# Two-layer hybrid trunk on one core: the big tiles of on-chip memory laid out in another order

## What is computed

```python
for l in range(DEPTH):                                   # DEPTH = 2
    x = x + 0.5 * swiglu(rmsnorm(x, ffn1_norm[l]), ffn1_w_gate[l], ffn1_w_up[l], ffn1_w_down[l])
    h = rmsnorm(x, mix_norm[l])
    proj = (h @ w_in[l]).astype(f32)
    z, xbc, dt_raw, q_raw, f_raw, i_raw, g_raw = jnp.split(proj, split_idx, axis=-1)
    y_ssd = ssd_mixer(z, xbc, dt_raw, ...)               # depthwise conv, chunked scan, gated norm
    y_hg = hgrn2_mixer(q_raw, f_raw, i_raw, g_raw, ...)  # gated linear recurrence by chunks
    x = x + jnp.concatenate([y_ssd, y_hg], axis=-1) @ w_out[l]
    x = x + 0.5 * swiglu(rmsnorm(x, ffn2_norm[l]), ffn2_w_gate[l], ffn2_w_up[l], ffn2_w_down[l])
return rmsnorm(x, final_norm)
```

## Time and profile before

| what | value |
|---|---|
| time, median of 3 runs | 2141.71 us |
| the three runs | 2128.27, 2141.71, 2146.33 us |
| the profiled execution: its own time | 2141.71 us |
| the profiled execution: its span | 2140.0 us |
| instructions of the span | 28388 |

### The profile page before, as it was taken

How to read it: one execution, slowest core, us unless ns; L and a number is a source line. 1 busy time by engine, 2 the same in 40 slices (tenths; PEclk the granted TensorE clock), 3 DMA queues, 4 the chain that set the end, 5 groups by cost and what they waited for, 6 DMA issues and landing times.

```text
span 2140.0 us, 28388 instructions
## 1 busy us (share of the span) xinstructions
PE 2093.1 (98%) x10300; PEld 1690.6 (79%) x10300; DVE 813.7 (38%) x1274; ACT 661.6 (31%) x903; POOL 848.1 (40%) x362
## 2 busy tenths in 40 slices
PE   8999999979999999999999999999899999999998
PEld 6888888856678888888888888887567788888887
DVE  7222211774477422221132222119645873222112
ACT  4322223422234322222332222224223342222232
POOL 4444444421123344444444444444211243444444
PEclk9999999988899999999999999999989999999999
DMA  4322232211111222233322223322101122222332
GB/s 146 111 97 92 90 100 91 91 49 40 35 55 60 89 98 92 94 93 99 103 90 98 98 97 92 98 77 89 50 32 49 59 80 89 98 92 95 98 92 95
DMA packets 55812, 181.61 MB, mean 85 GB/s; under 512 B 8368, under 2 KB 10416, under 8 KB 55728
## 3 DMA queue, kind: packets, MB, share of 16 engines
q1 hardware_dynamic: 55728, 180.52, 26.0%
HBM read 178.40 MB, written 2.10 MB: 84 GB/s over the span
## 4 chain that ended last, share of the span: by engine, by line
PE 91%; DVE 6%; issue 2%; DMA 0%; ACT 0%; SPq 0%; DVEq 0%; ACTq 0%
PE ps L1209 28%; PE ps L1210 27%; PE ps L1211 27%; PE ps L1367 3%; DVE acc L826 1%; PE ps L1406 1%; PE ps L1409 1%; PE ps L1459 1%; DVE xs L865 1%; PE ps L1462 1%; PE ps L1224 0%; DVE b L829 0%; DVE b L833 0%; DVE t L824 0%; PE ps L1484 0%
## 5 line engine op out<-in xcount | busy, mean ns | idle before, releaser
L412 POOL TENSOR_TENSOR wlo<-raw,whi 128x1024 fp32r<-128x1024 f32 x348 | 845.7, 2432 | 1280.7 <-ACT whi L445 717.3
L1209 PE MATMUL ps<-hhi,whi 128*128 128x512 f32 x1840 | 739.6, 402 | 0.2 <-issue 0.2
L1210 PE MATMUL ps<-hlo,whi 128*128 128x512 f32 x1840 | 727.2, 395 | 0.0
L1211 PE MATMUL ps<-hhi,wlo 128*128 128x512 f32 x1840 | 726.2, 395 | 0.0
L1209 PEld LDWEIGHTS ps<-hhi,whi 128*128 128x128 f32 x1840 | 352.0, 191 | 83.5 <-issue 9.5
L1211 PEld LDWEIGHTS ps<-hhi,wlo 128*128 128x128 f32 x1840 | 351.8, 191 | 75.3
L1210 PEld LDWEIGHTS ps<-hlo,whi 128*128 128x128 f32 x1840 | 351.9, 191 | 69.8
L445 ACT ACTIVATE whi<-raw 128x1024 fp32r<-128x1024 f32 x168 | 177.3, 1055 | 448.9 <-PE ps L1211 448.9
L1209 PE MATMUL ps<-ahi,whi 128*128 128x512 f32 x704 | 273.9, 389 | 0.0
L1210 PE MATMUL ps<-alo,whi 128*128 128x512 f32 x704 | 273.9, 389 | 0.0
L1211 PE MATMUL ps<-ahi,wlo 128*128 128x512 f32 x704 | 273.9, 389 | 0.0
(11 more groups left out here) (225 smaller groups left out, 1518.1 us busy)
## 6 DMA issues: line engine op xcount, KB each, us to landing
raw<-in_up SPq DMA_DIRECT2D x168, 512.0 KB, 3.2
raw<-in_mix SPq DMA_DIRECT2D x66, 512.0 KB, 3.3
raw<-in_dn SPq DMA_DIRECT2D x64, 448.0 KB, 3.3
raw<-in_dn SPq DMA_DIRECT2D x32, 512.0 KB, 3.5
raw<-in_lead SPq DMA_DIRECT2D x12, 512.0 KB, 3.2
stage<-in_x SPq DMA_DIRECT2D x4, 512.0 KB, 7.0
out<-stage SPq DMA_DIRECT2D x8, 256.0 KB, 2.9
raw<-in_mix SPq DMA_DIRECT2D x4, 256.0 KB, 2.5
```

Source lines behind the costliest of these rows:

```text
L412: pool.tensor_tensor(wlo[:, q, :], raw[:, q, :], whi[:, q, :].bitcast(F32), ALU.subtract).then_inc(split.sem, 1)
L1209: mm(dst, whi[:, q, s], mh, start=start, stop=False)
L1210: mm(dst, whi[:, q, s], ml, start=False, stop=False)
L1211: return mm(dst, wlo[:, q, s], mh, start=False, stop=stop)
```

## The change

The tile x is allocated ahead of hhi, and the arena behind all the other tiles instead of between hlo and x. Nothing else is edited. All lines of the file behind the arena's new place stand one line higher up: L1209 becomes L1208, and so on.

```diff
+        x = sb("x", [P, KD, T])
         hhi = sb("hhi", [P, KD, T], F32R)
         hlo = sb("hlo", [P, KD, T], F32R)
-
-
-        REGION = 27 * 1024 + 256 + 62 * 1024
-        arena = sb("arena", [P, REGION // 4])
-        base = nc.sbuf_base - REGION
-
-        x = sb("x", [P, KD, T])
         raw = sb("raw", [P, NS, BW])
         whi = sb("whi", [P, NS, BW], F32R)
         wlo = sb("wlo", [P, NS, BW], F32R)
...
         ntn = sb("ntn", [P, 2, TC * 8])
         headsum = sb("headsum", [P, NP * 8])
+
+
+        REGION = 27 * 1024 + 256 + 62 * 1024
+        arena = sb("arena", [P, REGION // 4])
+        base = nc.sbuf_base - REGION
```

## The result

The changed kernel took 2153.55 us in the median of 11 runs (2144.57 to 2166.11), the kernel before 2136.51 us in 11 runs (2128.27 to 2146.79). The ratio is 1.0067 with a 95% interval of 1.0042 to 1.0093: slower by 14 us on 2136.51, with 9 to 20 us as the interval. The two medians of 11 lie 17.0 us apart; over all 24 runs of the changed kernel on record, these 11 among them, the median is 2150.16 us, which is 13.7 above 2136.51. The forecast was 2141.7 us with a range from 2124 to 2151: 2153.55 lies 2.6 us above it. The change was forecast as nothing and is a small loss, within 1%.

The account below looks back on a forecast made before the run. PE (TensorE), busy 98% of the span and 91% of the chain, was taken to bound the kernel. All terms were 0, summing to 0 us on the profiled execution's 2141.71, so 2141.7 us, range 2124 to 2151.

Parts of the forecast that it names:

- the first term: The 7632 split-weight matmuls on PE's path: new addresses cost 0 ns each, with bounds of 13 ns either way.
- the slower rival: Down projection, 2112 matmuls: reads of ahi and alo starting mid 128-byte line cost 13 ns each, 27.5 us, 2169.2 us; chance 0.025.
- two signs that were to make it right: For the slower rival: mean for ahi of 399 ns or more, or 288 matmuls in 100 us of a down projection.
- The bounds of 13 ns on the matmuls: Split-weight matmuls: difference between the mean of 402 ns with hhi and 389 with ahi, taken as bound on both sides.
- The faster rival: Products with hhi and hlo: dearer by their places and cheaper once moved, 46.0 us, giving 2095.7 us; chance 0.015.
- The terms of DVE, ACT, POOL and the transfers: Work beside the matmuls: 0 each; bounds 0.3 us either way for DVE, 3.8 us for the last x load.
- The loads of x: Four transfers into stage, landing in 7.0 us: taken as 0; the skill's page would give 0.4 us to the good.
- The clock: PE's granted clock, mean 0.978, 47 us lost: drawn anew, over 1% either way to 2120.3 or 2163.1 us; chance 0.03.

Follow-up runs that it names:

- Experiment a: Changed kernel with 64 unused bytes ahead of the arena, so it is as high but starts at a multiple of 128; 2136.96 us, ratio to before 1.0011.
- f: Kernel before with 64 unused bytes ahead of hhi, so every large tile starts 64 past a multiple of 128; 2135.36 us, ratio 0.9983.
- d: Kernel before with whi and wlo, the stationary operands, moved to 64 past a multiple of 128; 2176.46 us in one run, against 2133.51 before.
- b: Kernel before with 64 unused bytes on either side of the arena, which also moved everything from x on by 128 bytes; 2170.68 us, ratio 1.018.
- k: Kernel before with hlo moved to 64 and alo to 128 behind whi and wlo, hhi and ahi at 0; 2170.33 us in one run, 2146.86 before.
- c: Kernel before with hhi at 0, hlo 32, ahi 64, alo 96 past a multiple of 128, whi and wlo moved by 128; 2150.07 us in one run.

## Why the prediction was wrong

**The step that failed is the first term,** the matmuls, with its "I take 0 ns each". It measured 6.6 ns on 2112 products, 13.9 us, and some 2.3 us on the 384 of w_out. Experiment a gives it back with 64 bytes, and with it the time. In absolute time a part of the miss is hidden by luck: the kernel before came to 2136.51 us in 11 runs, 5.2 below the 2141.71 from which the forecast started.

**How the rows misled.** The prediction looked for a price of a tile's own place. The earlier trace rows did show many places, but every one of them had the same distance modulo 256 to the weights, since the large tiles have 16384 bytes and the arena 91392, all multiples of 256, and each began where another ended. So these rows never varied what counts. The row that was to clear the 64 bytes, identr as the moving operand in the earlier trace rows, did have a distance of 64 to hlo, its stationary partner, and lm, with which it was compared, has one of 0 to xdt (both are in the arena, 24 KB apart). So it compared the right thing without meaning to, and the 272 and 273 ns are equal; but these are products of 128 columns, lm's with half the stationary columns, and the loss is in those of 512. acb_lo (L1433) has 512 columns but 8 partitions, and its stationary operand is one column of identr spread out, another one each time, at distances from 192 down to 164; with its 389 ns it too shows no loss. Both were taken for the nearest rows by place, where the pairing, in the same shape, was the thing to match.

In the changed kernel these rows moved a little too (L1432, L1592 and L1458; ns min/median/max): acb_lo from a median of 389 to 392, and identr beside hlo from 273 to 278, though their own distances modulo 256 are as before. The rule of the table is shown for the 128 x 128 by 128 x 512 products alone; what moved these isn't known.

```profile
L1432 PE MATMUL ps<-acb_lo,identr x16: 392/392/393, 569.4 to 1690.8; 8*128 8x512 f32 x16
...
L1592 PE MATMUL ps<-identr,hlo x32: 276/278/416, 2131.3 to 2140.2; 128*128 128x128 f32 x32
...
L1458 PE MATMUL ps<-lm,xdt x128: 272/273/324, 587.5 to 1708.8; 128*64 128x128 f32 x128
```

**What was right.** The place and the sign of the slower rival: the down projection, with the arena's start 64 bytes off. Its price was half of what was put on it (6.6 against 13 ns), and so it ended below the 10.1 ns from which it was to decide; with 0.025 it had too small a chance, and its mechanism, a line of 128 bytes, is refuted by f. Of the two signs that were to make it right, one came (288 matmuls of whi in 100 us of a down projection) and one didn't (a mean of 399 ns for ahi; it is 394): they stood for different prices. The bounds of 13 ns on the matmuls would have held the time, had they been carried into the range: 27.5 us over 2146 is 2174. The prediction stated them and then left them out. The faster rival is refuted by the counts of 443. The terms of DVE, ACT, POOL and the transfers were 0, and their rows stand still. The loads of x landed in 6.6 instead of 7.0 us; that is the size of the estimate from the Trainium skill's "DMA: Bandwidth & Descriptors", "How a descriptor splits into AXI transactions", but with one profile each it shows nothing, and PE's wait for them went from 9.6 to 9.1 us in all. The clock drew differently in the one profile, 6 us to the good, and by the medians of 11 runs that doesn't remain.

**What is shown and what isn't.** Shown: with any distance other than 0 modulo 256 that was tried, in steps of 32 bytes, PE's step for the products of 512 columns grows from 0.227 to between 0.229 and 0.234 us in the mean over the three products (d moves the weights against the moving tiles, a undoes the arena's shift, f moves all). That the remainder is taken by 256 rests on few values: modulo 512 the distance was 256 in the kernel before and is 0 for hhi and hlo in the changed one, with 443 both times, while 128 has 430 in b. Other engines and transfers aren't needed for the loss. In the trace of the changed kernel 245 of the 2111 steps with ahi and alo pass while no instruction of ACT, DVE or POOL and no transfer runs, and their mean is 233.2 ns; before, 218 such steps had 226.6. It isn't shown which two accesses of PE meet. PE's weight load for the next product runs beside the stream of the present one (187 ns within a step of 233), so a meeting of PE's own two reads is the likely reading, argued and not tested by a run without the weight load. The Trainium skill, in "SBUF — State Buffer" under "Who interferes with whom", gives PE two independent read ports, one for the moving operand and one for the weights, and says that PE never waits on anyone. The measurements differ as to the layout of tiles: in d PE's step grew from 227 to 233 ns by the place of the weights, so there that sentence can't be relied on. Why 64 costs 439 in one place and 430 in another stays open.

## What to carry to other kernels

When tiles are laid out, the starts of the moving and the stationary operands of dense matmuls like these should have one remainder modulo 256 bytes; a pad of 64 bytes was worth 0.7% here, and a shift of all tiles together nothing. A small tile allocated between two large ones is enough to spoil this, so the addresses are worth printing after each edit of the allocations. And a row clears an edit only if it varies what the edit varies, in the shape that matters: a place read many times at one relation to its partner says nothing of another relation.

## What the runs showed of the hardware

- PE's step for a 128 x 128 by 128 x 512 fp32r product at full clock was 226.7 ns with a distance of 0 between the two tiles' starts modulo 256, and 229 to 234 ns in the mean over the three products with any other distance tried, most often 233. The largest mean of a single product of the up and down projections was 235.8 ns, in k.
- The layout alone can cost 43 us: d has 2176.46 us in one run against 2133.51 of the kernel before, with not one instruction added or taken out.
- The loss is there with all other engines idle: 233.2 ns in 245 such steps of the changed kernel, 226.6 ns in 218 before.
- The cost isn't that of a pair alone: in k products with a distance of 0 took 230.0 to 235.8 ns beside one with 64 or 128. In c one product with a distance of 128 took 226 ns and another with the same distance 231.
